# A stream encoder step in float32: two block products change places, and the next part's row sums are made early

## What is computed

```python
def block_out(x, pool_o, attn_o, w_out, norm_ffn, w_gate, w_up, w_down):
    h = x + jnp.concatenate([pool_o, attn_o], axis=-1) @ w_out
    hn = rms_norm(h, norm_ffn)
    return h + (jax.nn.silu(hn @ w_gate) * (hn @ w_up)) @ w_down
```

## Time and profile before

| | |
|---|---|
| Three runs | 2154.95, 2160.76, 2159.62 us; median 2159.62 us |
| Profiled execution | 2159.57 us, span of its instructions 2157.8 us |
| Granted clock of PE, mean | 0.99 of full speed |
| PE, PEld busy | 97%, 88% of the span |
| DVE, ACT, POOL busy | 61%, 41%, 37% |
| DMA | 195.59 MB, mean 91 GB/s |

### The profile page before, as it was taken

The page is one execution under the profiler, slowest core; times in us unless marked ns, Lnnn a source line. Parts: engine busy times, 40 slices in busy tenths (PEclk is TensorE's granted clock), DMA queues, the critical chain, the costliest instruction groups (busy, mean ns, idle before and its releaser), DMA issues.

```text
span 2157.8 us, 33524 instructions
## 1 busy us (share of the span) xinstructions
PE 2091.9 (97%) x12454; PEld 1892.5 (88%) x12454; DVE 1320.9 (61%) x2214; ACT 884.7 (41%) x2149; POOL 797.5 (37%) x501
## 2 busy tenths in 40 slices
PE   6999999998999999999999999999999899999998
PEld 6888888876788899999998899999998899999997
DVE  5555656554123466675667866666677766766665
ACT  5666666643334533333333332333333433333331
POOL 1100000033324454444534644354445644444352
PEclk9999999999999999999999999999999999999999
DMA  6111111023675532222123432222223422221221
GB/s 182 30 38 38 41 40 40 23 68 100 216 237 170 166 98 78 79 79 79 60 79 106 166 105 63 78 76 79 79 79 95 162 73 79 79 79 59 79 79 74
DMA packets 236730, 195.59 MB, mean 91 GB/s; under 512 B 20749, under 2 KB 216122, under 8 KB 236570
## 3 DMA queue, kind: packets, MB, share of 16 engines
q1 hardware_dynamic: 236570, 193.46, 29.2%
HBM read 158.50 MB, written 35.03 MB: 90 GB/s over the span
## 4 chain that ended last, share of the span: by engine, by line
PE 88%; DVE 5%; ACT 2%; issue 2%; DMA 1%; POOL 1%; SPq 0%; DVEq 0%; ACTq 0%
PE ps L771 26%; PE ps L773 26%; PE ps L772 25%; PE ps L867 2%; PE ps L841 2%; PE ps L853 1%; PE ps L962 1%; PE ps L785 1%; DVE xs_lo L1485 1%; PE ps L964 1%; PE ps L960 1%; PE ps L829 1%; DVE xs_lo_raw L1480 1%; ACT s_sb L1115 1%; POOL w_lo L688 1%
## 5 line engine op out<-in xcount | busy, mean ns | idle before, releaser
L688 POOL TENSOR_TENSOR w_lo<-w_lo_raw,w_hi 128x512 fp32r<-128x512 f32 (+1 forms) x232 | 388.7, 1681 | 598.7 <-PE ps L773 414.8
L771 PE MATMUL ps<-xs_hi,w_hi 128*128 128x352 f32 x1848 | 597.8, 323 | 10.0 <-issue 5.3
L773 PE MATMUL ps<-xs_lo,w_hi 128*128 128x352 f32 x1848 | 597.9, 324 | 0.0
L771 PEld LDWEIGHTS ps<-xs_hi,w_hi 128*128 128x128 f32 x1848 | 348.0, 188 | 14.1 <-issue 12.6
L1604 DVE TENSOR_TENSOR h<-ps,h 128x512 f32<-128x512 f32 (+1 forms) x396 | 272.1, 689 | 134.4 <-PE ps L773 127.5
L773 PEld LDWEIGHTS ps<-xs_lo,w_hi 128*128 128x128 f32 x1848 | 351.0, 190 | 0.0
L772 PE MATMUL ps<-xs_hi,ws_lo 128*128 128x352 f32 x1056 | 339.5, 322 | 0.0
L688 POOL TENSOR_TENSOR ws_lo<-ws_lo_raw,w_hi 128x512 fp32r<-128x512 f32 x200 | 287.0, 1436 | 120.7 <-DVE ws_lo_raw L1453 76.3
L1182 ACT ACTIVATE w_hi<-ws_lo_raw 128x512 fp32r<-128x512 f32 x264 | 165.6, 627 | 337.2 <-DVE ws_lo_raw L1453 333.1
L771 PE MATMUL ps<-w_hi,act_hi 128*128 128x512 f32 x660 | 259.3, 393 | 10.0 <-issue 9.8
L772 PE MATMUL ps<-w_hi,act_lo 128*128 128x512 f32 x660 | 258.5, 392 | 0.0
(11 more groups left out here) (127 smaller groups left out, 3326.6 us busy)
## 6 DMA issues: line engine op xcount, KB each, us to landing
w_lo_raw<-in_w_gate SPq DMA_DIRECT2D x66, 512.0 KB, 5.1
w_lo_raw<-in_w_up SPq DMA_DIRECT2D x66, 512.0 KB, 5.1
w_lo_raw<-in_w_down SPq DMA_DIRECT2D x66, 512.0 KB, 4.1
xload<-in_x_prompt SPq DMA_DIRECT2D x16, 512.0 KB, 4.5
mix_d<-o_st SPq DMA_DIRECT2D x64, 128.0 KB, 1.8
xt_lo_raw<-mix_d SPq DMA_DIRECT2D x16, 512.0 KB, 6.5
wg_hi_raw<-in_x_prompt SPq DMA_DIRECT2D x16, 512.0 KB, 5.7
h_d<-wg_hi_raw SPq DMA_DIRECT2D x16, 512.0 KB, 2.8
```

The lines of the kernel that those rows point to most:

```text
L688: nc.gpsimd.tensor_tensor(lo, raw, hi.bitcast(F32), ALU.subtract).then_inc(done, 1)
L771: nc.tensor.matmul(out, s_hi, m_hi, start=first, stop=False, skip_group_check=partial)
L773: return nc.tensor.matmul(out, s_hi, m_lo, start=False, stop=final, skip_group_check=partial)
```

## The change

Products 4 and 5 change places: product 4 is now the one that uses the weight block (1, 1) and goes to bank 1, and product 5 goes to bank 2, where product 6 goes too. The results come in another order: c21 after product 4, c22 after product 5. `down` starts its first tiles when two of the four low parts are there instead of three. At a part's end ACT makes w_down's high parts one place earlier, and POOL makes its low parts in four pieces instead of two. The four row sums of the next part are made inside the part, at the ends of gate sets of groups 2, 4, 5 and 6, in two buffers (`turn_a`, `turn_b`), stored to a DRAM tensor `sums_d`, and loaded at the boundary; the two first blocks wait in the two buffers. All seven low parts of rows are now made by DVE. The core of the diff:

```diff
-BANK_OF = (0, 1, 2, 0, 2, 1, 2)
+BANK_OF = (0, 1, 2, 0, 1, 2, 2)
...
-A_BLOCK = {0: (0, 0), 3: (0, 1), 5: (1, 1)}
+A_BLOCK = {0: (0, 0), 3: (0, 1), 4: (1, 1)}
-RESULTS = ((0, 0), (1, 1), (1, 0), (0, 1))
+RESULTS = ((0, 0), (1, 0), (1, 1), (0, 1))
+        sums_d = nc.dram_tensor("sums_d", (PART, PARTS - 1, 4, HALF_K, NB), F32, kind="Internal").ap()
...
+            def next_rows(p, j):
+                a, b, done = turn_a[:, :, :], turn_b[:, :, :], 4 * (p - 1)
+                def store_sum(n, src):
+                    sp.wait_ge(x_sum, 4 * p + n + 1)
+                    sp.dma_start(sums_d[:, p - 1, n], src).then_inc(sums_stored, 16)
+                if j == 1:
+                    load(a, rows_block(p, 0, 1), turn_a_loaded)
+                    load(b, rows_block(p, 1, 1), turn_b_loaded)
+                elif j == 2:
+                    store_sum(0, b)
+                elif j == 3:
+                    sp.wait_ge(sums_stored, 16 * (done + 1))
+                    load(b, rows_block(p, 0, 0), turn_b_loaded)
+                elif j == 4:
+                    store_sum(1, a)
+                    load(b, rows_block(p, 1, 1), turn_b_loaded)
+                elif j == 5:
+                    sp.wait_ge(sums_stored, 16 * (done + 2))
+                    store_sum(2, b)
+                    load(a, rows_block(p, 1, 0), turn_a_loaded)
+                elif j == 6:
+                    sp.wait_ge(sums_stored, 16 * (done + 3))
+                    store_sum(3, a)
+                    load(b, rows_block(p, 0, 0), turn_b_loaded)
+                elif j == 7:
+                    sp.wait_ge(sums_stored, 16 * (done + 4))
+                    load(a, sums_d[:, p - 1, 0], turn_a_loaded)
+            def load_blocks(p):
+                for m, src in ((2, sums_d[:, p - 1, 2]), (3, rows_block(p, 1, 0)), (4, sums_d[:, p - 1, 3]),
+                               (5, sums_d[:, p - 1, 1]), (6, rows_block(p, 1, 1))):
+                    sp.wait_ge(product_done, after_product(last_set(p), m))
+                    load(xs_raw[:, m], src, block_loaded[m])
...
-                    sp.wait_ge(product_done, after_product(s - 2, 5))
+                    sp.wait_ge(product_done, after_product(s - 2, 4))
...
+                    next_rows(p + 1, j)
+                    if j == GROUPS - 1:
+                        load_blocks(p + 1)
...
+                need(pool, w_sum, 4 * s + (1, 2, 3, 3, 4, 4, 4)[m])
+            def low1(G, cuts=1):
+                    for n in range(cuts):
+                        cols = slice(1024 // cuts * n, 1024 // cuts * (n + 1))
+                        low(w1_high, 2 * G + c + 1, w1_lo[:, c, cols], w1_raw[:, c, cols], w1_hi[:, c, cols], w1_split)
...
                 for m in range(PRODUCTS):
                     low2(2 * G + 1, m)
-                    low1(G)
+                    low1(G, 2)
                     if p + 1 < PARTS:
                         pool.wait_ge(product_done, after_product(2 * G + 1, PRODUCTS - 1))
-                        for rows, m in ((1, 1), (0, 3), (0, 4), (1, 3), (0, 5), (1, 5), (0, 6)):
-                            if rows:
-                                rows_low(p + 1, m)
-                            else:
-                                low2(2 * G + 2, m)
+                        for m in range(3, PRODUCTS):
+                            low2(2 * G + 2, m)
...
+                    if p > 0:
+                        pe.wait_ge(xs_split_dve, 4 + PRODUCTS * (p - 1) + m + 1)
...
-                    pe.wait_ge((p1_saved, u2_ready, q7_ready, c22_read)[m - 3], s + 1)
+                    pe.wait_ge((p1_saved, q7_ready, u2_ready, c22_read)[m - 3], s + 1)
...
-                pe.wait_ge(w1_split, 2 * G + 2)
+                pe.wait_ge(w1_split, 2 * G + 2 + 2 * ((G + 1) // GROUPS))
-                    pe.wait_ge(al_done, 4 * G + (3 if PART * (j + 1) <= NB else 4))
+                    pe.wait_ge(al_done, 4 * G + (2 if PART * (j + 1) <= NB else 4))
...
-                if m in (1, 4, 2, 5):
-                    act.wait_ge(x_sum, 4 * p + (1, 4, 2, 5).index(m) + 1)
+                    if m == 0:
+                        act.wait_ge(turn_b_loaded, 16 * 4 * p)
+                    elif m == 1:
+                        act.wait_ge(turn_a_loaded, 16 * 3 * p)
+                    else:
+                        act.wait_ge(block_loaded[m], 16 * p)
...
-                    for m in range(3):
-                        high2(s + 1, m)
+                    high2(s + 1, 0)
+                    high2(s + 1, 1)
+                    if j < GROUPS - 1:
+                        high2(s + 1, 2)
                 high1(G)
+                if j == GROUPS - 1 and G + 1 < NG:
+                    high2(s + 1, 2)
                 if s == 1:
...
+                    for m in range(PRODUCTS):
                         rows_high(p + 1, m)
...
+            def next_rows_sum(p, n):
+                a, b = turn_a[:, :, :], turn_b[:, :, :]
+                dve.wait_ge(turn_a_loaded, 16 * (3 * (p - 1) + (1, 1, 1, 2)[n]))
+                dve.wait_ge(turn_b_loaded, 16 * (4 * (p - 1) + (1, 2, 3, 3)[n]))
+                out, other = (b, a) if n % 2 == 0 else (a, b)
+                nc.vector.tensor_tensor(out, out, other, ALU.subtract).then_inc(x_sum, 1)
...
             def rows_low(p, m):
-                dve.wait_ge(x_sum, 4 * p + (2 if m == 0 else 4))
-                dve.wait_ge(xs_high, PRODUCTS * p + X_HIGHS.index(m) + 1)
+                dve.wait_ge(xs_high, PRODUCTS * p + m + 1)
                 nc.vector.tensor_tensor(xs_lo[:, m], rows_raw(p, m), xs_hi[:, m].bitcast(F32), ALU.subtract)\
                     .then_inc(xs_split_dve, 1)
...
-                m = (4, 5, 6)[n - 1]
+                m = n + 3
-                dve.wait_ge((q7_ready, u2_ready, p1_saved)[n - 1], s + 1)
+                dve.wait_ge((u2_ready, q7_ready, p1_saved)[n - 1], s + 1)
-                nc.vector.tensor_tensor(out, product_bank(s, m), (q7[:, :], u2[:, :], p1[:, s % 2, :])[n - 1], ALU.add)\
-                    .then_inc((c22_read, c21_read, c12_read)[n - 1], 1)
+                nc.vector.tensor_tensor(out, product_bank(s, m), (u2[:, :], q7[:, :], p1[:, s % 2, :])[n - 1], ALU.add)\
+                    .then_inc((c21_read, c22_read, c12_read)[n - 1], 1)
...
+                (p, j), now = divmod(s // 2, GROUPS), s % (2 * GROUPS) == 0
+                    rows_low(p, 5)
                 result_sum(s, 1)
+                result_sum(s, 2)
                 if now:
                     weight_sum(s + 1, 3)
-                result_sum(s, 2)
                 result_sum(s, 3)
+                if p + 1 < PARTS and j in (2, 4, 5, 6):
+                    next_rows_sum(p + 1, (2, 4, 5, 6).index(j))
...
                 low_part(G, 0)
                 act_product(G, 1)
+                result_sum(s, 2)
+                low_part(G, 1)
                 if more:
                     weight_sum(s + 1, 3)
-                result_sum(s, 2)
-                low_part(G, 1)
                 act_product(G, 2)
...
                 for j in range(PT_TILES):
-                    if j < 4:
-                        if group < GROUPS - 1:
-                            weight_sum(2 * G + 3, j)
-                        elif p + 1 < PARTS:
-                            rows_sum(p + 1, j)
-                    elif group == GROUPS - 1 and p + 1 < PARTS:
-                        rows_low(p + 1, X_LOWS_DVE[j - 4])
+                    if j < 4 and group < GROUPS - 1:
+                        weight_sum(2 * G + 3, j)
+                    elif j > 0 and group == GROUPS - 1 and p + 1 < PARTS:
+                        rows_low(p + 1, j - 1)
```

More of the change, by code:

```diff
@@ L82 @@
 W_LOW = {e: i for lows in W_LOWS.values() for i, e in enumerate(lows)}
[L84 to L86 removed]
+X_HIGHS = (0, 1, 5, 2, 3, 4, 6)
+X_LOWS_DVE = (0, 2, 5, 6)
+X_LOWS_POOL = (1, 3, 4)
+X_SUMS = (1, 5, 2, 4)
 def rows_of(t):
@@ L296, in build @@
         xs_loaded = sem("xs_loaded")
[L297 to L300, removed]
+        turn_a_loaded = sem("turn_a_loaded")
+        turn_b_loaded = sem("turn_b_loaded")
+        block_loaded = [sem(f"block_loaded{m}") for m in range(PRODUCTS)]
         w2_loaded = [sem(f"w2_loaded{i}") for i in range(2)]
@@ L433, in raw_of @@
                 return w2_raw[s % 2][:, i, j]
-            return ws_raw[:, {1: 0, 2: 1, 4: 2, 6: 3 + s % 2}[m]]
+            return ws_raw[:, {1: 0, 2: 1, 5: 2, 6: 3 + s % 2}[m]]
         def rows_raw(p, m):
-            return b22[:, :, :] if m == 6 and p > 0 else xs_raw[:, m]
+            if p > 0 and m < 2:
+                return (turn_b, turn_a)[m][:, :, :]
+            return xs_raw[:, m]
         def d_index(G, j, nh=0):
@@ L565, in load_first_rows @@
                 rows_stored(0)
-                for m, j, l in ((0, 0, 0), (4, 0, 1), (3, 1, 0), (6, 1, 1)):
+                for m, j, l in ((0, 0, 0), (5, 0, 1), (3, 1, 0), (6, 1, 1)):
                     load(xs_raw[:, m], rows_block(0, j, l), xs_loaded)
[L569 to L581, removed]
```

(13 more changed lines are left out.)

73 lines of the change are left out of this document (30 added, 43 removed).

## The result

The changed kernel takes **2224.58 us** (median of 4 runs, 2223.05 to 2227.8); the kernel before took 2160.19 us in the runs beside it. The ratio is 1.0305, 95% interval [1.0286, 1.0325]: slower by 64.4 us, where 50 were forecast. The time lies inside the prediction's 2190 to 2226 us, at the upper end, but that end stood for boundaries without a gain, and they did gain: what brought the time there is a term that the sum does not have. One execution of the version of experiment 9 took 9245 us, stands outside its ratio, and no trace says why. The profiled execution of the change took 2227.8 us, 3.2 us above that median, with a span of 2226.0 us.

The account below looks back on a forecast made before the run. PE was taken to bound the kernel, busy 97% of the span and dense between boundaries. From 2159.6 us, +58.3 (swap), -6 (boundaries) and -1.2 (end) gave 2210.7, stated as 2210 us; range 2190 to 2226.

Parts of the forecast that it names:

- The wait ahead of product 6: Every gate and up set: product 6 waits for DVE's sum behind product 5; 0.94 us a set, 62 sets, +58.3 us.
- the rule that the prediction cites from the Trainium skill: TensorE's queue can pull weight loads ahead of matmuls in flight; would lower the wait 0.07 us a set, some 4 us.
- The weight sum that stood there is moved behind it: Up sets: DVE's weight sum goes behind the sum after product 5, so 0.94 us holds for gate and up sets alike.
- DVE or ACT a little late: Reason for the upper bound of product 6's wait: 1.0 us a set, +62 us in all.
- The boundaries: Sets 21 to 23 and 43 to 45: early row sums pay after down; -3 us each, -6 in all.
- the steps: First boundary, from set 21's start: product 6 near 15.2 us, down(10) near 18.6, down's end near 36, set 23 near 53.
- the 1.5 us that the steps price for a slow clock: Boundary product 6, behind a 3.5 us wait: half speed for about 3 us, so 1.5 us lost.
- The end: Down(32) no longer waits for the third low part: -1.2 us, bounds -1.3 and 0.
- The rest: Row sums at gate sets' ends, added DMAs and SP's later weight loads: priced at nothing; uncovered row sums +10 at most.
- no boundary of 45 us: Rival: boundaries come clean, product 6 not held, set 23 begins near 45 us, -11 each, 2195 us; chance 0.2.
- a clock of 1.00 between the boundaries: Answers the rival that the clock falls at every new wait: 66 x 1.5 us on top, 2310 us; chance 0.05.
- no cover for the wait: Answers the rival "not slower": product 6's wait mostly covered, under 0.43 us a set; chance 0.05.

Follow-up runs that it names:

- experiment 9: experiment 1's version, next part's first weights between down's additions, then last-tile additions and weight sums moved behind the sum releasing product 6: 2141.61 us, ratio 0.9913.
- experiment 3: Kernel before, with product 6 also waiting for the sum behind product 5, which it does not need; nothing else changed: 2226.16 us, ratio 1.0299.
- experiment 5: Changed kernel with only ACT's copy of product 0 of the next gate set moved ahead of the last high part: 2210.31 us, ratio 1.0232.
- experiment 6: Changed kernel with the third result's 64-column DVE instruction moved behind the last multiplication: 2209.38 us, ratio 1.0227.
- experiment 1: Changed kernel with the swap of products 4 and 5 undone, the rest of the change kept: 2149.52 us, ratio 0.9957.
- experiment 4: Changed kernel with ACT's copy of product 0, and the next weight high part with it, moved ahead of the last activation high part: 2254.72 us, ratio 1.0436.

## Why the prediction was right or wrong

**The wait ahead of product 6: right.** 0.87 us, and 0.08 us for the longer step from the first matmul behind it to the next, in every ordinary set, gate and up alike, at full clock; experiment 3 shows it alone. The weight load of the waiting matmul began at 1301.62 us in set 25, 0.03 us ahead of its matmul, as in the earlier trace rows; the rule that the prediction cites from the Trainium skill, "TensorE: Matmul & The Clock Gate" (section "Architectural detail: the array is 16× 32×32, not 1× 128×128"), is again not borne out for a load behind a wait. In the 61 sets outside the boundaries and set 0 it sums to 53.3 us, and to about 58 with the longer step behind it, which is the term of 58.3.

**The step that failed** is the part on the swap's order on DVE: "The weight sum that stood there is moved behind it", with "DVE or ACT a little late" as the bound. The sum has no term for any wait but that of product 6: I followed DVE's list to the awaited sum and stopped there. Behind it the swap makes a result with a 64-column tail the third, so that small instruction moves behind product 6, where POOL runs. One more turn, 1.26 us for the last multiplication, goes through ACT's list to its copy of product 0, and product 3 of the next gate set waits. Measured, 0.49 us and 0.08 us for the longer step, 30 times: 17 us, or the 14 to 15 that experiments 5 and 6 win back. It covers the missing 14 us. That 2210 us come out once this wait is gone is partly luck: in the profiled execution of the change the boundaries and the end won 4.8 us more than forecast, and the mixer ahead of the FFN and sets 0 and 1 took 4.6 us more than the two waits priced there.

**The boundaries: right in mechanism, too small in size.** Set 21 went by the steps. PE at the first boundary of the change, and three stretches of it (product 6 of set 21, down(10), set 22):

```profile
1208.48 0.63 PE L803 MATMUL ps<-xs_hi,w_hi 128*128 128x352 f32 x1 [3.04 <-DVE aa L1552]
...
1212.13 0.63 PE L803 MATMUL ps<-w_hi,act_hi 128*128 128x512 f32 x1
```

```profile
1208.40:1212.10 3.70, 3.62 (x12) 3.65 (x13) 1.56 (x3) 1.56 (x4) 0.00 (x0) 0.50 0.36 145
1212.10:1229.00 16.90, 16.80 (x70) 13.06 (x70) 16.06 (x19) 9.90 (x9) 5.34 (x4) 0.94 0.65 216
1229.00:1244.60 15.60, 13.60 (x86) 13.34 (x85) 14.07 (x18) 5.05 (x10) 5.35 (x4) 1.00 0.70 223
```

Product 6 started at 14.7 us (forecast 15.2), ran at a clock of 0.50, and down(10) began at 18.4 us (18.6). Down and set 22 then took 32.5 us where the steps gave 34.4: down ended 0.8 us early, and set 22 took 15.6 us, not 17: it lost 2.2 us, nearly all of it ahead of product 6, and its row low parts came in time. At the second boundary product 6 waited as long, but ran at a clock of 1.00, so the 1.5 us that the steps price for a slow clock were not lost there (the rows stand in the last section). So -5.1 and -5.6 us, not -3 each.

**The end: right.** Down(32) starts 0.16 us after the last matmul of set 65; the earlier trace rows had 1.42.

**The rest.** The rivals fell as argued: no boundary of 45 us, a clock of 1.00 between the boundaries behind 20 + 10 short waits, and no cover for the wait. The early row sums and their DMAs cost nothing that shows: experiment 1 carries them and is dense at 423.10 us. In the profiled execution the mixer ahead of the FFN, which the change leaves almost as it was, took 2.5 us more; in experiment 3, whose mixer is that of before, it took 2.1 us more, so executions scatter by this much. Sets 0 and 1 took 4.0 us more, and 4.1 in experiments 4 and 6, but 0.8 us more in experiment 5, whose lists are the same in set 0. There set 0 took 19.16 us at a granted clock of 1.00, in the change 22.86 us at 0.79, and in the kernel before 19.76 us at 0.91. So the clock of set 0 makes most of that difference; what decides the clock stays open.

## What to carry to other kernels

Where an accumulator is read and then added to, keep a product on another bank between the two: here that read cost PE 0.95 us in each ordinary set, since nothing covered it. Follow a reordered list past the wait you are pricing, through every engine it feeds, to the next thing PE waits for; here an instruction of 64 columns, moved to where POOL runs, cost 0.98 us instead of 0.23, and by way of ACT 17 us in all. And before a boundary, put work that isn't due for 20 or 30 us behind what the next product waits for.

## What the runs showed that I had not expected

A 64-column instruction with two SBUF inputs took 0.23 us alone and 0.98 us beside POOL, where it ended 0.1 us after POOL's first piece of 1.27 us, so its price there is POOL's piece and not its own length. The Trainium skill, "SBUF — State Buffer" (section "🔬 SBUF: two separate sides"), says that a DVE instruction with two SBUF inputs and a GpSimd one that reads SBUF hold one pair of ports in turn, each for its whole instruction; these rows agree.

And the clock after a wait is not told by the wait's length: product 6 of set 21 waited 3.0 us and then ran at 0.50, the lower of the clock's two levels, for 3.7 us, while product 6 of set 43 waited as long and ran at 1.00. Its first matmul, its stretch, and the stretch of product 6 of set 44:

```profile
1706.88 0.40 PE L803 MATMUL ps<-xs_hi,w_hi 128*128 128x352 f32 x1 [3.04 <-DVE aa L1552]
...
1706.80:1708.86 2.06, 1.99 (x13) 2.02 (x13) 1.56 (x3) 0.95 (x4) 0.00 (x0) 1.00 0.73 293
...
1739.30:1742.50 3.20, 3.18 (x12) 3.20 (x13) 0.69 (x1) 1.41 (x3) 3.20 (x4) 0.59 1.08 362
```

There the low clock (last row) came in set 44, behind a wait of 2.0 us. What decides between the two stays open.
